# Eight attention pairs written out instead of looped, the last two units of two output projections interleaved, and a copy moved ahead of another

## What is computed

```python
for layer in range(2):
    xn = rms_norm(h, g_mix[layer])
    if layer == 0:                       # two convolution mixers, 1024 channels out
        h = h + mixers(xn @ w_in_ab) @ w_out_ab
    else:                                # 16 heads x 64, three dilated windows, ALiBi, merged
        q, k, v = qkv_split(xn, w_qkv)
        h = h + dilated_attention(q, k, v) @ w_o
    xn = rms_norm(h, g_ffn[layer])       # ConvFFN, D_FF = 2816
    z = xn @ w_ffn_in
    h = h + (silu(conv3(z[:, :D_FF])) * z[:, D_FF:]) @ w_down
y = rms_norm(h, g_final)
```

## Time and profile before

| what | value |
|---|---|
| median of 3 runs | 2820.11 us (2817.78 to 2821.62) |
| the profiled execution, its own time | 2819.68 us |
| its span, first to last instruction | 2817.8 us |
| TensorE matmuls busy | 2627.1 us (93%), x17426 |
| VectorE / GpSimd / ScalarE busy | 1443.6 / 779.9 / 621.4 us |
| mean granted TensorE clock | 0.973 of full speed |
| projections and gates, L618 | 1485.3 us busy, 100.5 us idle before |

### The profile page before, as it was taken

How to read it: one execution, slowest core, us unless ns; L and a number is a source line. 1 busy time by engine, 2 the same in 40 slices (tenths; PEclk the granted TensorE clock), 3 DMA queues, 4 the chain that set the end, 5 groups by cost and what they waited for, 6 DMA issues and landing times.

```text
span 2817.8 us, 43027 instructions
## 1 busy us (share of the span) xinstructions
PE 2627.1 (93%) x17426; PEld 2471.6 (88%) x17426; DVE 1443.6 (51%) x2014; ACT 621.4 (22%) x909; POOL 779.9 (28%) x432
## 2 busy tenths in 40 slices
PE   6978588999999999999989899979899999999996
PEld 6878588999999999997777777758899999999995
DVE  5999933444444444465555555661444444444444
ACT  4100133111111111133333333342311111111111
POOL 5323323432323232341101100123243333333332
PEclk9988799999999999999999999999999999999998
DMA  5442255444444444544434343434111111111111
GB/s 192 157 156 89 89 76 182 164 164 165 164 165 164 165 164 165 208 164 156 165 121 165 136 143 134 157 106 147 38 50 48 44 48 45 47 46 46 45 42 62
DMA packets 93884, 337.00 MB, mean 120 GB/s; under 512 B 22528, under 2 KB 39808, under 8 KB 91136
## 3 DMA queue, kind: packets, MB, share of 16 engines
q1 hardware_dynamic: 93696, 334.20, 34.9%
HBM read 315.88 MB, written 152.25 MB: 166 GB/s over the span
## 4 chain that ended last, share of the span: by engine, by line
PE 70%; issue 13%; DVE 13%; POOL 2%; ACT 1%; DMA 0%; POOLq 0%; DVEq 0%; SPq 0%
PE reg L618 43%; PE reg L634 18%; DVE g L1325 6%; PE reg L762 4%; DVE spare L1325 2%; PE reg L742 1%; POOL acc L1169 1%; PE ob L798 1%; POOL w_sp L392 1%; PE reg L783 1%; DVE nmx L1534 1%; PE ob L783 1%; PE reg L851 0%; DVE neg_s L1529 0%; DVE prod L1333 0%
## 5 line engine op out<-in xcount | busy, mean ns | idle before, releaser
L618 PE MATMUL reg<-xs,w_sp 128*128 128x352 f32 x8928 | 1485.3, 328 | 100.5 <-DVE xs L1294 36.5
L618 PEld LDWEIGHTS reg<-xs,w_sp 128*128 128x128 f32 x8928 | 1471.4, 191 | 112.9 <-issue 87.4
L372 POOL TENSOR_TENSOR w_sp<-w_raw,w_sp 128x1024 fp32r<-128x1024 f32 x172 | 430.6, 2504 | 1066.7 <-ACT w_sp L367 1065.5
L634 PE MATMUL reg<-hid,w_sp 128*128 128x352 f32 x3168 | 514.4, 323 | 0.0
L634 PEld LDWEIGHTS reg<-hid,w_sp 128*128 128x128 f32 x3168 | 511.5, 188 | 0.2 <-DVE tmp L1469 0.2
L367 ACT ACTIVATE w_sp<-w_raw 128x1024 fp32r<-128x1024 f32 x172 | 182.5, 1061 | 1215.7 <-PE reg L618 810.7
L1305 DVE TENSOR_TENSOR h<-reg,h 128x1056 f32<-128x1056 f32 x192 | 241.4, 1258 | 370.5 <-PE reg L634 234.4
L762 PE MATMUL reg<-xs,w_sp 128*128 128x352 f32 x1512 | 282.2, 334 | 13.5 <-issue 13.5
L1435 DVE TENSOR_TENSOR g<-reg,rst 128x1056 f32<-128x1056 f32 x44 | 55.4, 1260 | 423.9 <-PE reg L618 423.8
L762 PEld LDWEIGHTS reg<-xs,w_sp 128*128 128x128 f32 x1512 | 242.9, 190 | 31.4 <-issue 31.3
L392 POOL TENSOR_TENSOR w_sp<-w_raw,w_sp 128x1024 fp32r<-128x1024 f32 x21 | 49.8, 2373 | 496.2 <-ACT w_sp L387 477.3
(11 more groups left out here) (161 smaller groups left out, 1684.7 us busy)
## 6 DMA issues: line engine op xcount, KB each, us to landing
w_raw<-in_wstream SPq DMA_DIRECT2D x193, 512.0 KB, 3.3
out_sk<-in_cache_k SPq DMA_DIRECT2D x16, 4088.0 KB, 16.2
out_sv<-in_cache_v SPq DMA_DIRECT2D x16, 4088.0 KB, 17.1
kvr<-in_kva SPq DMA_DIRECT2D x16, 2048.0 KB, 9.0
kvr<-in_kvb SPq DMA_DIRECT2D x16, 1536.0 KB, 6.8
wt<-in_wtab SPq DMA_DIRECT2D x16, 512.0 KB, 5.3
h<-in_xT SPq DMA_DIRECT2D x4, 1056.0 KB, 10.5
h_spill<-h SPq DMA_DIRECT2D x8, 528.0 KB, 2.6
```

Of the source, the lines that this page charges most:

```text
L372: nc.gpsimd.tensor_tensor(w_sp[:, u % 3, 1, :], w_raw[:, u % 3, :], w_sp[:, u % 3, 0, :].bitcast(F32), ALU.subtract).then_inc(w_lo, 1)
L618: mm = nc.tensor.matmul(out[:, t, :], w[:, wh, k * P:(k + 1) * P], xs[:, xh, k, t * TS:(t + 1) * TS], start=(n == 0 and wh + xh == 0), sto ...
L634: mm = nc.tensor.matmul(out[:, t, :], w[:, wh, kk * 512 + m * P:kk * 512 + (m + 1) * P], hid[:, par_g, kk, xh, t * TS:(t + 1) * TS], start ...
```

## The change

Three things are changed. The loop over pairs is gone on all five engines, and `Pair` holds a plain number. The seventh and eighth unit of `U_OUT` and `U_WO` are no longer two `in_proj` calls but one `last_two`, which goes through the chunks once and gives each chunk to both units; after each chunk it counts `x_free`, and ScalarE and VectorE rewrite that chunk of `xs` for the ConvFFN while the projection is still running. And in step 0 of a pair `vnew` is copied before `vrow`.

```diff
-        def pairs(eng, body):
-
-            with eng.Fori(0, NPAIR // 2 - 1) as i:
-                body(Pair(i, 0))
-                body(Pair(i, 1))
-            body(Pair(None, NPAIR - 2))
-            body(Pair(None, NPAIR - 1))
+        def pairs(body):
+
+            for p in range(NPAIR):
+                body(Pair(p))
...
+            def last_two(u, r):
+
+                for x in range(2):
+                    pe.wait_ge(w_lo, cnt(u + x))
+                open_use(r)
+                for k in range(KD):
+                    for x in range(2):
+                        if k == 0 and x == 1:
+                            open_use(r + 1)
+                        out, w = region(r + x), w_sp[:, (u + x) % 3]
+                        for wh, xh in ((0, 0), (0, 1), (1, 0)):
+                            for t in range(NT):
+                                mm = nc.tensor.matmul(out[:, t, :], w[:, wh, k * P:(k + 1) * P],
+                                                      xs[:, xh, k, t * TS:(t + 1) * TS],
+                                                      start=(k == 0 and wh + xh == 0), stop=(k == KD - 1 and wh == 1))
+                        if k == KD - 1:
+                            mm.then_inc(full, 1)
+                        elif x == 1:
+                            mm.then_inc(x_free, 1)
...
-            for m in range(2, KD):
+            for m in range(2, KD - 2):
                 in_proj(U_OUT + m, FIRST[U_OUT + m], order=mix)
+            last_two(U_OUT + KD - 2, FIRST[U_OUT + KD - 2])
...
+            def new_x(L, m):
+
+                s, e = (1, 2) if L == 0 else (3, 5)
+                if m < KD - 1:
+                    act.wait_ge(x_free, (KD - 1) * L + m + 1)
+                else:
+                    act.wait_ge(full, LAST[(U_OUT, U_WO)[L] + KD - 1] + 1)
+                h_ready(act, s, m)
+                gain_hi(s, e, m)
...
             for m in range(KD):
+                if m == KD - 2:
+                    for x in range(KD - 2):
+                        new_x(0, x)
                 hi_after(act, U_OUT + m)
+                if m >= KD - 2:
+                    new_x(0, m)
                 h_ready(act, 1, m)
                 square(1, m, h[:, m, :])
...
             for m in range(KD):
+                if m == KD - 2:
+                    for x in range(KD - 2):
+                        gain_lo(1, 2, x)
                 add_to_h(FIRST[U_OUT + m], m)
+            for m in range(KD - 2, KD):
+                gain_lo(1, 2, m)
...
                         dve.wait_ge(ta_full, pr.n(T_VROW + 1, NTA))
+                        dve.wait_ge(ss_full, pr.n(PHASE[0] + 1, NPH))
+                        nc.vector.tensor_copy(vnew[:, :], S[0][0:NS, 0:P]).then_inc(ss_free, 1)
                         nc.vector.tensor_copy(vrow[:, 0:4, :],
                                               TP[0].rearrange("p (t c) -> p t c", c=P)).then_inc(ta_free, 1)
-                        dve.wait_ge(ss_full, pr.n(PHASE[0] + 1, NPH))
-                        nc.vector.tensor_copy(vnew[:, :], S[0][0:NS, 0:P]).then_inc(ss_free, 1)
```

More of the change, by code:

```diff
@@ L152, with __init__ @@
 class Pair:
-    def __init__(self, i, c):
-        self.i, self.c, self.par = i, c, c % 2
-        self.last = i is None and c == NPAIR - 1
+    def __init__(self, p):
+        self.p, self.par, self.last = p, p % 2, p == NPAIR - 1
     def n(self, k, per):
-        return at(k + self.c * per, self.i, 2 * per)
+        return k + self.p * per
     def slot(self, x):
-        return 1 + (3 * self.c + x + 1) % 2
+        return 1 + (3 * self.p + x + 1) % 2
     def landed(self, x):
[L166 to L173, removed]
+        k = 3 * self.p + x
+        return k % 2, 16 * (k // 2 + 1)
 def build(nc, xT, wstream, par, ident_d, ones_d, stA, stB, stF, kva, kvb, wtab, sbias, cache_k, cache_v,
@@ L545, in pair @@
                     sp.wait_ge(sc_free, pr.n(2 * CHUNK0[4] + 1, 2 * NCH))
-                    load_table(0, pr.row(wtab[0], 1))
-                if pr.i is not None:
+                    load_table(0, wtab[0][pr.p + 1])
+                if pr.p < NPAIR - 2:
                     load_qkv(sp, pr, 4)
@@ L899, in _ @@
             pe.wait_ge(d_free, 3)
-            scores(Pair(None, 0), 0, 0)
-            pairs(pe, pair)
+            scores(Pair(0), 0, 0)
+            pairs(pair)
             pe.wait_ge(ta_free, NTA * NPAIR + 1)
             pe.wait_ge(o_free, 2 * NPAIR + 1)
-            for m in range(KD):
+            for m in range(KD - 2):
                 in_proj(U_WO + m, FIRST[U_WO + m], x_at=4 * KD if m == 0 else None, part=(KD - 1,) if m == 0 else range(KD))
+            last_two(U_WO + KD - 2, FIRST[U_WO + KD - 2])
             ffn(1)
@@ L1130, in pair @@
                 outputs(0)
-            first = Pair(None, 0)
+            first = Pair(0)
             act.wait_ge(zero_ok, 1)
@@ L1138, in _ @@
             nc.scalar.activation(w_sp[:, first.slot(0), 0, :], w_raw[:, first.slot(0), :], ACT.Copy).then_inc(aw_hi, 1)
-            pairs(act, pair)
+            pairs(pair)
             act.wait_ge(o_free, 2 * NPAIR + 1)
@@ L1252, in pair @@
                                                 ALU.subtract).then_inc(x_lo, 1)
-            qkv_lo(pool, Pair(None, 0), 0)
-            pairs(pool, pair)
+            qkv_lo(pool, Pair(0), 0)
+            pairs(pair)
             split_lo(pool, U_WO + 2)
@@ L1412, in _ @@
             for m in range(KD):
+                if m == KD - 2:
+                    for x in range(KD - 2):
+                        gain_lo(1, 2, x)
                 add_to_h(FIRST[U_OUT + m], m)
+            for m in range(KD - 2, KD):
+                gain_lo(1, 2, m)
             def ffn(L):
-                s, e = (1, 2) if L == 0 else (3, 5)
-                for m in range(KD):
-                    gain_lo(s, e, m)
                 factor_parts((5, 9)[L])
@@ L1625, in _ @@
             project(2, reg[0][:, :, 0:TS], VT)
-            neg_scores(Pair(None, 0), 0, 0)
-            pairs(dve, pair)
+            neg_scores(Pair(0), 0, 0)
+            pairs(pair)
             dve.wait_ge(x_hi, 4 * KD + KD)
@@ L1636, in _ @@
             for m in range(KD):
+                if m == KD - 2:
+                    for x in range(KD - 2):
+                        gain_lo(3, 5, x)
                 add_to_h(FIRST[U_WO + m], m)
+            for m in range(KD - 2, KD):
+                gain_lo(3, 5, m)
             ffn(1)
```

51 lines of the change are left out of this document (19 added, 32 removed).

## The result

The changed kernel takes 2786.93 us (median of 4 runs, 2782.04 to 2789.57) against 2820.0 us before (2817.78 to 2821.62): a ratio of 0.9882, 95% interval 0.987 to 0.9894. I had forecast 2785.5 us and a range of 2780 to 2796. The profiled execution has a span of 2785.0 us. On another chip the same kernel took 2788.41 us against 2819.63, a ratio of 0.9886.

The account below looks back on a forecast made before the run. TensorE was taken as the bound, its matmuls busy 93% of the span. From the profiled 2819.7 us, -16.3 - 17.9 + 0 = -34.2 us gave 2785.5 us, range 2780 to 2796.

Parts of the forecast that it names:

- Part 1: Attention pair loop written out: two jumps back, each with 6.80 us of TensorE idle and slower work behind, go; -16.3 us.
- The ruler: Time between `vnew` copies of successive pairs: 85.98 and 85.96 us over a jump, 77.82 us straight.
- rival that the gap is not the jump's: At the pair loop's jumps, the idle has another cause; writing out gains at most 2.2 us, 2799.6 us; 4%.
- Part 2: Output projection to ConvFFN seams: interleaving the last two units removes 7.22 us idles and slow units; -17.9 us net.
- the one mis-sized term of the sum: Layer 0, before `last_two`: TensorE stands for the eighth unit's late weights; +1.8 us, no clock fall.
- the row of 3.20 us at a clock of 1.00: Old profile at 1846.20: TensorE almost idle without a clock fall, taken to show that short standstills keep the clock.
- the weights of layer 0 come later than before: Sign of a wrong prediction: the eighth unit's weight split in layer 0 ends after the old 437.11.
- The sum of squares: At the seam, after the first ConvFFN unit: ready before TensorE asks for it, so no wait.
- its cover: At the seam, time to spare between the sum of squares being ready and TensorE asking for it: 2.2 us.
- the rival: At both seams, slowed GpSimd makes the sum of squares late and the clock may fall; 2795.7 us; 9%.
- Part 3: Step 0 of each pair, `vnew` copied first: 0 us, since TensorE then waits for `norm` before `turn`; bound -5.5.
- Starved straight code: At all seven pair boundaries, the `kvr` fill holds up straight code's instructions, 8.15 us each; 2842.6 us; 2%.

Follow-up runs that it names:

- e1: Only the loop over pairs written out, against the kernel before; 2803.93 us, ratio 0.9947.
- e4: Kernel before, loop kept, SyncE's next-pair `kvr` fill and what it issues after moved behind the jump back; 2814.52 us, ratio 0.9978.
- Part 2 alone: Only the two seams changed (`last_two`), pairs still looped, against the kernel before, run twice; 2808.25 and 2805.92 us, ratios 0.9955 and 0.9947.
- e3: Only the copy order changed (`vnew` before `vrow`), against the kernel before; 2819.97 us, ratio 0.9999.
- e12: Changed kernel with the `kvr` fill issued behind the next pair's first sample phase; 2788.37 us, beside 2788.41 for the changed kernel.
- e2: Only the two seams changed (`last_two`), pairs still looped, against the kernel before, first run; 2808.25 us, ratio 0.9955.
- e11: The changed kernel run once more, on another chip; 2788.41 us, ratio 0.9886 to the kernel before.
- e6: Changed kernel with GpSimd's second weight split of each seam done twice; 2791.6 us, ratio 0.9897 to the kernel before.
- e7: Changed kernel with the ConvFFN loops of the four compute engines also written out; 2777.75 us, ratio 0.9851 to the kernel before.

## Why the prediction was right

**Part 1**, -16.3 us: 16.5 us in the profile from the first pair to the eighth, 16.8 us alone (e1). The ruler, pair lengths with and without a jump, measured the idle stretch and the slower clock behind it in one number, and it could be carried over as it was. The rival that the gap is not the jump's fell with e1 and e4. One reading was too narrow: the DMA engines were not busy with the fill of `kvr` alone in the stretch, but with two stores and a weight load as well (e4). The Trainium skill ("Advanced Engine Details and Errata", Control Flow Timing) has about 108 ns for a compare-and-branch. The runs show more for the whole jump: with nearly idle DMA engines TensorE still stood 3.3 us here, and 0.6 to 1.3 us at the jumps of the ConvFFN loops. Why the ConvFFN's jump is the cheaper one was not tried.

**Part 2**, -17.9 us, is right in its mechanism. Layer 1's seam gave 9.3 us of the 9.5 and layer 0's 10.1 of the 10.2 before its wait. That wait is the one mis-sized term of the sum: I put it at +1.8 us from one profile's landing time and took no fall of the clock. It measured 0.76 to 4.30 us in seven profiles, 2.56 in the middle one, and in six of them, with waits of 2.23 us and more, the clock fell as well; the whole cost was 4.0 us in the middle and 6.5 at most. So the row of 3.20 us at a clock of 1.00 was the wrong guide. Part 2 alone was worth 12.5 and 13.7 us. The first profile of the changed kernel had the shortest wait of the seven: that part of the close agreement is luck. With 4.0 in place of 1.8 the forecast would have been 2787.7 us; the two medians are 2786.93 and 2788.41. The prediction had also named as a sign of being wrong that the weights of layer 0 come later than before (437.1). They did in three of the seven profiles, by 0.4 to 0.7 us.

**The sum of squares** was named as next, and is; but its cover is 0.6 us and not 2.2. I had added durations of GpSimd's operations from stretches without VectorE's low parts beside them; with them, one add took 3.05 us and one split 3.40, together 1.6 us more than I had put in, which is the cover that is missing. That the add kept its ordinary time beside the low parts in the old seam did not carry over. The rows with 3.47 and 3.56 us, which I used for the rival, were the better guide.

**Part 3**, 0 us: e3 measured a ratio of 0.9999, and the waits traded places as described.

**Starved straight code**: no straight boundary shows a wait of the matmuls for "issue", in any of the kernels with written-out pairs (e12 has one of 0.66 us inside its eighth pair), and the fill of `kvr` may be early or late (e12).

## What to carry to other kernels

When an idle stretch stands at a loop's jump back, compare one passage with a straight one, and look at what bulk transfers are in the queue at that moment: here writing the loop out removed the stretch, and moving the transfers behind the jump removed half of it. When work is interleaved to close a seam, a wait that two pieces used to make at two times is now made at the earlier one, so ask when the later piece's data landed, and how much that varies. Moving a copy ahead in one engine's queue gives nothing if the reader's next need is at that queue's end.

## What the runs showed of the hardware

The lower clock follows short standstills more readily than I had read from one row. In the earlier trace rows 3.2 us with TensorE almost idle left the clock at 1.00; a standstill of 4.30 us (e2) had it at 0.78 on the mean, and at 0.50 for the 4.87 us of full work behind it. In e11 a wait of 2.23 us between two stretches of dense matmuls kept 1.00 while it lasted, and the lower level came in the work behind it:

```profile
432.35:434.58 2.23, 0.01 (x1) 0.03 (x1) 1.26 (x1) 1.23 (x2) 2.23 (x2) 1.00 1.49 618
434.58:438.00 3.42, 3.42 (x13) 3.42 (x14) 0.00 (x0) 1.47 (x2) 3.42 (x2) 0.55 1.00 384
```

The two units took 24.95 us instead of 23.4, some 1.5 us more. The waits of 2.39, 2.56 and 2.58 us in e6, e12 and e7 were followed by a mean clock of 0.58, 0.53 and 0.50 in the work right behind them. No run shows why the 3.2 us of the earlier trace rows were spared.

Single-element work on VectorE is held up by GpSimd too. The kernel's 128x1 minimum (L1534 before, L1552 after) took 1.7 to 2.4 us instead of 0.16 in the last pair, where GpSimd subtracts 128x1056 tiles at the same time. Timeline of GpSimd and VectorE in the last pair of the kernel before:

```profile
1854.76 4.85 POOL L1251 TENSOR_TENSOR xs<-att,xs 128x1056 fp32r<-128x1056 f32 x2 [7.25 <-ACT xs L1060]
1855.30 1.91 DVE L1534 TENSOR_TENSOR nmx<-nmx 128x1 f32<-128x1 f32 x1
1857.91 1.72 DVE L1534 TENSOR_TENSOR nmx<-nmx 128x1 f32<-128x1 f32 x1
```

The two subtracts fill 4.85 us, so the first ends near 1857.2 and the second at 1859.61; the two minima end at 1857.21 and 1859.63. The Trainium skill ("SBUF — State Buffer", SBUF: two separate sides) says that a VectorE instruction with two SBUF inputs and a GpSimd instruction that reads SBUF share a port pair, which the one that starts first holds for its whole instruction while the other is blocked. The trace agrees with it here, though no run took GpSimd's work away to show it.
